# Two-layer decoder step: the Strassen weight sums kept in DRAM, products accumulated in a bank, and pool mixing with float32 products

## The reference

```python
def multiscale_pool(u_ext, pos, w_group, scale):
    ...
    for g, w in enumerate(POOL_WINDOWS):
        ...
        outs.append((end[..., sl] - start) / cnt)
    pooled = jnp.concatenate(outs, axis=-1)
    d = (pooled - u_ext[:, POOL_HIST:].astype(jnp.float32)).astype(u_ext.dtype)
    y = jnp.einsum('btgc,gcd->btgd', d.reshape(b, t, POOL_GROUPS, POOL_GC), w_group)
    return y.reshape(b, t, c) * scale

def reference(...):
    for l in range(DEPTH):
        h_p, h_s = rmsnorm(y_p, norm_pre[l]), rmsnorm(y_s, norm_pre[l])
        mk_p, mv_p = mem_kv(mem_prompt, mem_norm[l], w_mem_kv[l])
        if l % 2 == 0:
            q, k, v, lf, xq_p, g_p = split_fox(h_p @ fox_w_in, fox_b_f)
            mix_p = fox_prompt(q, k, v, lf)
            ...
        else:
            u_p, xq_p, g_p = split_pool(h_p @ pool_w_in)
            mix_p = multiscale_pool(u_ext_p, jnp.arange(t), pool_w_group, pool_scale)
            ...
        y_p = y_p + rmsnorm(gated_out(mix_p, mem_attend(xq_p, mk_p, mv_p), g_p, w_out[l]), norm_post[l])
```

## Time and profile before

| | |
|---|---|
| Three runs | 3430.72, 3435.74, 3435.37 us; median 3435.37 |
| The profiled execution | 3434.42 us, its span 3432.6 us |
| Mean granted TensorE clock | 0.974 of full speed |
| Busy: PE, PEld, DVE, ACT, POOL | 3208.1, 2781.0, 1576.7, 1247.2, 764.1 us |
| HBM read, written | 408.96, 129.99 MB |

### The profile page before, as it was taken

The page is one execution under the profiler, slowest core; times in us unless marked ns, Lnnn a source line. Parts: engine busy times, 40 slices in busy tenths (PEclk is TensorE's granted clock), DMA queues, the critical chain, the costliest instruction groups (busy, mean ns, idle before and its releaser), DMA issues. The chain is left out here.

```text
span 3432.6 us, 53641 instructions
## 1 busy us (share of the span) xinstructions
PE 3208.1 (93%) x19865; PEld 2781.0 (81%) x19865; DVE 1576.7 (46%) x2934; ACT 1247.2 (36%) x2411; POOL 764.1 (22%) x922
## 2 busy tenths in 40 slices
PE   7999999999999999999999999987988988776999
PEld 7999999777777777788888888876978887674887
DVE  4232223232333226555555543327766786775332
ACT  4112232223222225455656641215553544322211
POOL 3310000001111112333334310004442453441000
PEclk9999999999999999999999999998999999997999
DMA  5435443679999854422322234414744433556431
GB/s 158 139 115 163 145 119 108 191 251 301 309 313 317 262 175 127 158 87 81 95 84 84 92 123 141 131 58 161 264 145 138 157 131 133 177 183 198 143 108 55
DMA packets 417761, 542.04 MB, mean 158 GB/s; under 512 B 53383, under 2 KB 300744, under 8 KB 416079
## 3 DMA queue, kind: packets, MB, share of 16 engines
q1 hardware_dynamic: 394663, 470.90, 43.4%
q0 software_dynamic: 22848, 67.78, 6.0%
HBM read 408.96 MB, written 129.99 MB: 157 GB/s over the span
## 5 line engine op out<-in xcount | busy, mean ns | idle before, releaser
L719 PE MATMUL bank<-t_hi_p,w_hi_p 128*128 128x352 f32 (+1 forms) x1008 | 338.0, 335 | 66.5 <-DVE t_lo_p L650 22.8
L719 PE MATMUL bank<-t_lo_p,w_hi_p 128*128 128x352 f32 (+1 forms) x1008 | 332.2, 330 | 0.0
L719 PE MATMUL bank<-t_hi_p,w_lo_p 128*128 128x352 f32 (+1 forms) x1008 | 331.9, 329 | 0.0
L2306 PE MATMUL bank<-w_hi_o,b_hi_o 128*128 128x512 f32 x782 | 305.7, 391 | 16.5 <-DVE w_lo_o L2232 16.5
L395 PE MATMUL bank<-h00hi,w_hi_p 128*128 128x352 f32 x960 | 317.4, 331 | 4.0 <-DVE h00lo L1522 3.1
L395 PE MATMUL bank<-h00hi,w_lo_p 128*128 128x352 f32 x960 | 309.3, 322 | 0.0
L395 PE MATMUL bank<-h00lo,w_hi_p 128*128 128x352 f32 x960 | 309.1, 322 | 0.0
L2307 PE MATMUL bank<-w_hi_o,b_lo_o 128*128 128x512 f32 x782 | 305.3, 390 | 0.0
L2308 PE MATMUL bank<-w_lo_o,b_hi_o 128*128 128x512 f32 x782 | 305.2, 390 | 0.0
L1192 PE MATMUL bank<-pT_fa,v_fa 128*128 128x256 f32 x1092 | 272.1, 370 | 4.4 <-issue 2.4
L395 PE MATMUL bank<-h01hi,w_hi_p 128*128 128x512 f32 x640 | 267.2, 417 | 0.0
(11 more groups left out here) (396 smaller groups left out, 7102.3 us busy)
## 6 DMA issues: line engine op xcount, KB each, us to landing
k_raw_sf<-in_cache_fox_k SPq DMA_DIRECT2D x128, 512.0 KB, 5.3
v_raw_sf<-in_cache_fox_v POOLq DMA_DIRECT2D x128, 512.0 KB, 5.9
w_raw_p<-in_fox_w_in SPq DMA_DIRECT2D x80, 512.0 KB, 4.9
w_raw_p<-in_pool_w_in SPq DMA_DIRECT2D x36, 1024.0 KB, 5.3
z<-z_st_p SPq DMA_DIRECT2D x64, 512.0 KB
b_raw_o<-bT SPq DMA_DIRECT2D x32, 768.0 KB, 6.3
z<-z_st_p SPq DMA_DIRECT2D x48, 352.0 KB, 2.6
out<-tok_p SPq DMA_DIRECT2D x64, 256.0 KB, 4.1
```

The lines of the kernel that those rows point to most:

```text
L719: last = nc.tensor.matmul(bank[:, 0:wd], st, mv, start=(m == 0 and i in (A11, S2, S3, S1)), stop=(m == 3 * KH - 1), skip_group_check=True)
L2306: nc.tensor.matmul(bank(t, half)[:, :], bh, w_hi, start=(k == 0), stop=False)
```

## The change

`weight_sums` is a new work of the first pass: it forms the four sums of each of the 12 pairs once, in 24 half units, and stores them with the quarters in DRAM as `ws`. The second pass loads all seven operands of a pair from there (1792 KB), one pair ahead. Its products are reordered (S4 of a pair comes behind A11 of the next), and A11, S2, S3, A22 of a pair accumulate in one bank and A12 on a copy of A11's product in another, S1 and S4 in a third; ScalarE reads out five partial results, VectorE adds twice. Pool mixing multiplies in float32 without splitting, and VectorE sums both channel halves.

```diff
-                pool.dma_start(ptab[:, :], page_table.rearrange("(o b) n -> o (b n)", o=1)).then_inc(pt_in, 16)
-                pool.wait_ge(pt_in, 16)
+                pool.dma_start(ptab[:, :], page_table.rearrange("(o b) n -> o (b n)", o=1)).then_inc(past_in, 16)
+                pool.wait_ge(past_in, 16)
...
-                pool.wait_ge(past_in, 16 * DB * PAGES)
+                pool.wait_ge(past_in, 16 + 16 * DB * PAGES)
             beside.advance(0)
...
+def weight_sums(nc, stack, tag, base, w, pairs, ws, plan):
...
+    KH, KC = KT // 2, 2
...
+    st = nc.alloc_sbuf_tensor_at(f"st_{tag}", [P, 7, KC, P], F32, offset=base)
+    a21 = nc.alloc_sbuf_tensor_at(f"a21_{tag}", [P, KC, P], F32, offset=base + 4 * 7 * KC * P)
...
+    units = [(q, n) for q in range(len(pairs)) for n in range(NC)]
+    NU = len(units)
+    STEPS = 2 * NU + 2
+    w_v = w.rearrange("(k p) n -> p k n", p=P)
+
+    def sp(sp):
+        for i in range(STEPS):
+            u = (i - 1) // 2
+            if i % 2 and u < NU:
+                q, n = units[u]
+                if u:
+                    sp.wait_ge(out_d, 16 * u)
+                for kind, tile, kh in ((A11, 0, 0), (A12, 0, 1), (A22, 1, 1), (None, 1, 0)):
+                    dst = a21[:, :, :] if kind is None else st[:, kind, :, :]
+                    k, col = KH * kh + KC * n, pairs[q] + tile * P
+                    sp.dma_start(dst, w_v[:, k:k + KC, col:col + P]).then_inc(q_in, 16)
+            if i % 2 == 0 and i:
+                u = i // 2 - 1
+                q, n = units[u]
+                sp.wait_ge(sum_d, 4 * (u + 1))
+                sp.dma_start(ws[q, :, :, KC * n:KC * (n + 1), :], st[:, :, :, :]).then_inc(out_d, 16)
+            if i == STEPS - 1:
+                sp.wait_ge(out_d, 16 * NU)
+            yield
+
+    def pool(pool):
+        for i in range(STEPS):
+            u = (i - 1) // 2
+            if i % 2 and u < NU:
+                pool.wait_ge(q_in, 64 * (u + 1))
+                for n, (to, a, b, op) in enumerate(((S1, a21[:, :, :], st[:, A22, :, :], ALU.add),
+                                                    (S3, st[:, A11, :, :], a21[:, :, :], ALU.subtract),
+                                                    (S2, st[:, S1, :, :], st[:, A11, :, :], ALU.subtract),
+                                                    (S4, st[:, A12, :, :], st[:, S2, :, :], ALU.subtract))):
+                    if n >= 2:
+                        pool.wait_ge(sum_d, 4 * u + (1 if n == 2 else 3))
+                    nc.gpsimd.tensor_tensor(st[:, to, :, :], a, b, op).then_inc(sum_d, 1)
+            yield
+    return Work(STEPS, plan, dict(sp=sp, pool=pool))
...
+    for q in range(NJ):
+        jobs += [(q, A11)] + ([(q - 1, S4)] if q else []) + [(q, S2), (q, A12), (q, S3), (q, S1), (q, A22)]
+    jobs.append((NJ - 1, S4))
...
-                    sp.wait_ge(wlo_d, 7 * (q - 2) + A22 + 1)
-                    sp.wait_ge(sum_d, 4 * (q - 1))
-                col = columns[2 * (q % NP)][0]
-                sp.dma_start(w_raw[:, q % 2, :, :], w_v[:, :, col:col + 2 * P]).then_inc(w_in[q % 2], 16)
+                    sp.wait_ge(wlo_d, place[q - 2, S4] + 1)
+                sp.dma_start(w_raw[:, q % 2, :, :, :], ws[q % NP]).then_inc(w_in[q % 2], 16)
...
+                if half == 0 and i == A11 and 1 <= q < NJ - 1:
+                    load(q + 1)
...
+                if i not in (S1, S4):
                     return
-                wd, u, bank = width(q), q % 2, accumulator(m)
-                v1, u2, u3 = (part[:, n, 0:wd] for n in range(3))
-                out, a, made = {S2: (u2, v1, 0), S3: (u3, u2, 1), S1: (z_st[:, u, 1, wd:2 * wd], u3, 2),
-                                A22: (z_st[:, u, 1, 0:wd], u2, 0), S4: (z_st[:, u, 0, wd:2 * wd], u2, 0)}[i]
-                if i == S2:
-                    dve.wait_ge(act_d, 2 * q + 1)
-                    if q:
-                        dve.wait_ge(dve_d, 5 * q)
...
-                if i in (S1, S4) and q >= 2:
+                wd, u, tile = width(q), q % 2, 1 if i == S1 else 0
+                dve.wait_ge(act_d, 5 * q + (4 if i == S1 else 2))
...
                     if i == A11 and q:
-                        pe.wait_ge(act_d, 2 * q)
-                    elif i == A12:
-                        pe.wait_ge(act_d, 2 * q + 1)
-                    elif i in (S2, S3) and q:
-                        pe.wait_ge(dve_d, 5 * (q - 1) + (4 if i == S2 else 5))
-                    elif i in (S1, A22, S4):
-                        pe.wait_ge(dve_d, 5 * q + {S1: 1, A22: 2, S4: 3}[i])
+                        pe.wait_ge(act_d, 5 * (q - 1) + 3)
+                    if i == S2:
+                        pe.wait_ge(act_d, 5 * q + 1)
+                    if i == A12:
+                        pe.wait_ge(act_d, 5 * q + 1)
+                    if i == S3:
+                        pe.wait_ge(act_d, 5 * q + 2)
+                    if i == A22:
+                        pe.wait_ge(act_d, 5 * q + 4)
+                    if i == S1 and q:
+                        pe.wait_ge(dve_d, 2 * q)
+                    if i == S4:
+                        pe.wait_ge(dve_d, 2 * q + 1)
...
-                    last = nc.tensor.matmul(bank[:, 0:wd], st, mv, start=(m == 0 and i in (A11, S2, S3, S1)),
+                    last = nc.tensor.matmul(bank, st, mv, start=(m == 0 and i in (A11, S1)),
                                             stop=(m == 3 * KH - 1), skip_group_check=True)
...
                 if i == A11:
-                    act.wait_ge(z_done, m + 1)
                     if q:
-                        act.wait_ge(dve_d, 5 * (q - 1) + 1)
-                    nc.scalar.copy(part[:, 0, 0:wd], bank[:, 0:wd]).then_inc(act_d, 1)
-                if i == A12:
-                    act.wait_ge(z_done, m + 1)
+                        act.wait_ge(act_d, 5 * q)
+                    nc.scalar.copy(accumulator(q, A12), accumulator(q, i)).then_inc(act_d, 1)
+                if i in (S2, S3):
                     if q >= 2:
-                        act.wait_ge(z_out[q % 2], stored(q - 2))
-                    nc.scalar.activation(z_st[:, q % 2, 0, 0:wd], bank[:, 0:wd], func(q)).then_inc(act_d, 1)
+                        act.wait_ge(dve_d, 2 * (q - 2) + 2)
+                    nc.scalar.copy(part[:, u, 0 if i == S2 else 1, 0:wd], accumulator(q, i)).then_inc(act_d, 1)
+                if i in (A12, A22):
+                    if q >= 2 and i == A12:
+                        act.wait_ge(z_out[u], stored(q - 2))
...
-                        wh, wl = wg_hi[:, g, ct, dt * P:(dt + 1) * P], wg_lo[:, g, ct, dt * P:(dt + 1) * P]
-                        nc.tensor.matmul(Y_BANKS[dt][:, :], wh, d_hi[:, ct, :], start=(ct == 0), stop=False)
-                        nc.tensor.matmul(Y_BANKS[dt][:, :], wh, d_lo[:, ct, :], start=False, stop=False)
-                        last = nc.tensor.matmul(Y_BANKS[dt][:, :], wl, d_hi[:, ct, :], start=False, stop=(ct == CT - 1))
+                        last = nc.tensor.matmul(Y_BANKS[dt][:, :], wg[:, g, ct, dt * P:(dt + 1) * P], dd[:, n % 2, ct, :],
+                                                start=(ct == 0), stop=(ct == CT - 1))
...
-                src = u[:, n % 2, 0, :]
+                src = u[:, n % 2, :, :]
...
-                    dst = acc[k % 2][:, 0, :]
-                    nc.vector.tensor_tensor(dst[:, lo:], src[:, lo:], src[:, lo - 2 ** k:Z + CN - 2 ** k], ALU.add).then_inc(sum_v, 1)
+                    dst = acc[k % 2][:, :, :]
+                    nc.vector.tensor_tensor(dst[:, :, lo:], src[:, :, lo:], src[:, :, lo - 2 ** k:Z + CN - 2 ** k], ALU.add).then_inc(sum_v, 1)
...
-                nc.vector.scalar_tensor_tensor(dd[:, :, :], last[:, :, Z:], 1.0 / w, u[:, n % 2, :, Z:], ALU.mult, ALU.subtract).then_inc(d_d, 1)
+                if n >= 2:
+                    dve.wait_ge(y_d, CT * (n - 1))
+                nc.vector.scalar_tensor_tensor(dd[:, n % 2, :, :], last[:, :, Z:], 1.0 / w, u[:, n % 2, :, Z:], ALU.mult, ALU.subtract).then_inc(d_d, 1)
...
-                nc.vector.tensor_tensor(d_lo[:, :, :], dd[:, :, :], d_hi[:, :, :].bitcast(F32), ALU.subtract).then_inc(dl_d, 1)
...
+    ws = scratch("ws", (len(POOL_TILES) // 2, P, 7, KT // 2, P))
...
+                sums = weight_sums(nc, sems, "ws", chunk0.base + 4 * 2 * D, pool_w_in, [t[0] for t in POOL_TILES[::2]], ws, [(2, 0), (40, 50)])
...
-                             [making, norm, kv, sample, gates, fox, prompt, late, head], (page_table, cache_logf, past, ptab), left)
+                             [making, norm, kv, sample, gates, fox, prompt, late, head, sums], (page_table, cache_logf, past, ptab), left)
...
-                                 [(31.6, 0), (33.4, 12), (34.4, 14), (35.4, 16), (35.99, 17)],
+                                 [(31.6, 0), (33.8, 12), (34.8, 14), (35.8, 16), (35.99, 17)],
```

236 lines of the change are left out of this document (93 added, 143 removed).

## The result

The changed kernel takes 3499.56 us (median; runs from 3495.29 to 3501.7), the kernel before 3435.36: the ratio is 1.0188, 95% interval 1.0171 to 1.0206, so it is slower by 64 us. The profiled execution took 3501.7 us, its span 3500.1, against 3434.42 and 3432.6 before: 67.5 us more in the span. That is less than the stall alone cost; the second pass gave half of it back.

The account below looks back on a forecast made before the run. TensorE bounds the first pass and VectorE, by the waits, paces the second. A stall of +128 and second-pass gains of -4, -35, -29 and -12 sum to +48 on 3434.4, giving 3482 us, range 3446 to 3520.

Parts of the forecast that it names:

- The likeliest case: Whole kernel: the first-pass stall outweighs the second pass's gains, 3482 us, given 74%.
- The block of SyncE, +128: First pass: SyncE waits for GpSimd's sums behind its gate loop; TensorE stalls 126 us, plus 2 for the clock.
- Later steps cost nothing on the path: First pass: weight-sum units after the stall add nothing to the time; the upper end allowed 10 us.
- The argument about weights two tiles ahead: First pass: weights loaded two tiles, 24 us, ahead cover a later unit's wait of about 12 us.
- Opening, -4: Second pass, 2311 to 2360 us: quicker operand builds against a larger load, 4 us saved, ends +2 and -10.
- Pairs 1 to 30, -35: Second pass, 2360 to 2943 us: freed VectorE recovers half the idle and 9 us of clock; ends -10 and -60.
- hidden, except behind other transfers: Second pass: the weight load lands in 7.1 us, against some 13 us until TensorE needs it.
- Waits on ScalarE: Second pass: new waits of products on ScalarE's copies cost 5 us in all, ends 0 and 48.
- Rival C: Second pass: saved VectorE time returns as waits on ScalarE's copies and the larger load, 48 us, total 3530; 10%.
- Mixing beside the products, -29: Second pass, 2943 to 3090 us: TensorE's 107 us and a tenth give 118 instead of 147; ends -10 and -40.
- Tail, -12: Mixing behind the last product: 29 us instead of 40.8, ends -5 and -16.
- `w_lo` at 0.69 throughout: Second pass: each `w_lo` on VectorE takes near 0.69 us, 71 us less over 252 of them.

Follow-up runs that it names:

- e1: Changed kernel with the plan of the weight sums at positions 15 to 44 instead of 2 to 40; 3381.47 us, ratio 0.9859.
- e12: e9 with no weight-sum steps between positions 19 and 20.6 and the second pass's first weight load in two parts; 3374.16 us, ratio 0.9828.
- e9: e1 with the load of `h_raw` in the slot of S1 instead of A11 and later token sums on VectorE instead of GpSimd; 3372.60 us, ratio 0.9827.
- e6: e1 with the sums of the later token groups on VectorE instead of GpSimd; 3376.56 us, ratio 0.9831.

## Why the prediction was right

The likeliest case came true, with its sign, its mechanism and a measured 3499.6 inside 3446 to 3520, 18 us above the forecast. By its own steps:

- **The block of SyncE, +128.** Right in every link: stop behind the load of tile 6, release by GpSimd's fourth sum, TensorE dry at 105.1 us. The release came at 215.9, not 220, as the loop ended 4 us earlier (last issue 211.0); the sums took 0.73 us each, not 0.65. TensorE went on at 226.13 instead of 230.8, and the lower clock added 2.4 us (12 matmuls at 0.43 instead of 0.23) where I had 2. Behind the stall the pass is 123.5 us late.
- **"Later steps cost nothing on the path"** was wrong: 6.6 us more at one place, the opening of the sample attention, as e1 and e12 show. That the sum came out at 130.7, close to 128, is luck: two errors of opposite sign. The argument about weights two tiles ahead was right and beside the point; the thin reserve was `tok`, with three buffers, and loads that ScalarE waits for in its queue.
- **Opening, -4:** -5.5.
- **Pairs 1 to 30, -35: the step that failed,** -17.1. The freed VectorE paid where it was the limit (the pairs at a change of group, 20 us). It was freed by less than I had: `w_lo` fell by 44 us, not 71. What I did not ask is what each moved transfer and sum now meets: the weight load comes one pair ahead and right before the load of `h_raw`, and a key load lands 16.0 us behind its issue (5.6 is the median). I had written "hidden, except behind other transfers" and put no price on the exception. It is 7.6 of the 12 us lost in pairs 9 to 13, shown by e9; 4 are open, and so are the other 6 between -35 and -17.
- **Waits on ScalarE:** 4.7 + 2.9 us on `part_p` and the copy of the bank, against 5. Rival C had its mechanism at a sixth of its price.
- **Mixing beside the products, -29:** -36.4, of which 3.7 us are only the stage's start (150.7 us before, where I had 147). TensorE was busy 110.8 of 115 us; the tenth that I added for hand-over was not needed, and the clock rose to 0.99 from the earlier trace rows's 0.88. My counts for the stretch were wrong both ways: from 2943 to 3090 us the trace before has 405 matmuls of products and 134 of the mixing, that is 33.8 products and 11.2 units, not 31 and 13. TensorE's sum comes to 107 either way, by luck. The products in float32 came as worked out: two records of 0.43 us for 512 columns. The sums took 1.25, as I took them.
- **Tail, -12:** -5.6. An arithmetic slip: four units stood behind the last product, and I summed three and the last products. The one left out, three sums, `dd` and two mixes, lasts 6.3 us (3167.17 to 3173.47), and with it 29 becomes 35, against 35.0 from 3160.44 on.
- **`w_lo` at 0.69 throughout:** the median is 0.693, the mean 0.803. GpSimd still makes the token sums; with these on VectorE (e6) the mean is 0.735, so they are over half of the difference.

## What to carry to other kernels

A work that one engine starts and another finishes puts a wait into an in-order queue; before it goes in, list what the finishing engine is busy with at that time, and what is queued behind the wait on both engines, down to the smallest memset. The cure here was the place in the plan, one line, not less work. And when an edit that removes a visible wait changes nothing, compare the stages pair by pair: two causes can hide each other, and only both edits together show their worth, here in the stage's time before the whole time could show it.

## What was not expected of the hardware

A VectorE subtraction of 128x512 with both inputs in SBUF took 3.22 us (up to 3.71) instead of 0.69 beside a GpSimd sum of 3.6 us, while VectorE's additions from a bank beside it kept their 0.49. And the 1792 KB load landed after 8.1 us (median of 36) where the slope of the earlier trace rows gave 7.1, while its first 512 KB, issued by themselves, were cast 3.7 us behind their issue.
